# mLSTM exponentials between broadcast copies, and old-state products of two heads in turn

## The reference

```
dmat = where(causal, b[t] - b[s] + li[s], -inf)
inter = b + m
m_t = maximum(inter, max(dmat))
a = exp(dmat - m_t) * (q @ k.T)
num = exp(inter - m_t) * (q @ C) + a @ v
den = exp(inter - m_t) * (q @ n) + sum(a)
h = num / maximum(abs(den), exp(-m_t))
```

## Time and profile before

| | us |
|---|---|
| median of the timed runs | 2559.96 (one run of 2558.49) |
| the profiled execution | 2559.59 |
| its span in the trace | 2557.8 |
| PE busy | 2479.5 (97% of the span) |
| DVE, ACT, POOL busy | 1115.5, 827.9, 1349.7 |

### The profile page before, as it was taken

How to read it: one execution, slowest core, us unless ns; L and a number is a source line. 1 busy time by engine, 2 the same in 40 slices (tenths; PEclk the granted TensorE clock), 3 DMA queues, 4 the chain that set the end, 5 groups by cost and what they waited for, 6 DMA issues and landing times.

```text
span 2557.8 us, 41382 instructions
## 1 busy us (share of the span) xinstructions
PE 2479.5 (97%) x17104; PEld 2327.7 (91%) x17104; DVE 1115.5 (44%) x1610; ACT 827.9 (32%) x1517; POOL 1349.7 (53%) x635
## 2 busy tenths in 40 slices
PE   5999999999999999999989999999999999999997
PEld 3989976888999999999978999679899999999997
DVE  4443375534355423132564526653353463222235
ACT  3261355435422303021223513553454122112031
POOL 2645530445566666666656356016445666666664
PEclk9999999999999999999999999999999999999999
DMA  6202234531122222222211022442111222222221
GB/s 268 75 19 74 77 108 166 197 107 42 50 75 75 66 76 75 75 78 74 79 60 58 30 80 78 148 149 79 61 44 59 75 71 78 75 76 75 75 75 58
DMA packets 62619, 214.63 MB, mean 84 GB/s; under 512 B 6816, under 2 KB 11360, under 8 KB 62176
## 3 DMA queue, kind: packets, MB, share of 16 engines
q1 hardware_dynamic: 56160, 202.92, 23.5%
q10 hardware_dynamic: 6272, 9.07, 1.0%
HBM read 207.14 MB, written 4.49 MB: 83 GB/s over the span
## 4 chain that ended last, share of the span: by engine, by line
PE 92%; DVE 3%; ACT 1%; DVEq 1%; DMA 1%; issue 1%; SPq 1%; POOL 0%; POOLq 0%; ACTq 0%
PE big L567 22%; PE big L570 22%; PE big L571 22%; PE four L753 6%; PE big L828 2%; PE big L776 2%; PE four L649 2%; PE four L859 2%; PE four L974 2%; PE four L840 2%; PE four L798 1%; PE big L595 1%; PE big L599 1%; PE big L598 1%; PE big L950 1%; DMA first_mod<-in_first 1%
## 5 line engine op out<-in xcount | busy, mean ns | idle before, releaser
L527 POOL TENSOR_TENSOR w_hi<-raw,cst 128x1024 fp32r<-128x1024 f32 (+1 forms) x286 | 547.9, 1916 | 1042.2 <-PE big L567 833.0
L530 POOL TENSOR_TENSOR w_lo<-raw,w_hi 128x1024 fp32r<-128x1024 f32 (+1 forms) x286 | 735.3, 2571 | 40.7
L567 PE MATMUL big<-act_hi,w_hi 128*128 128x320 f32 x2304 | 718.6, 312 | 5.1 <-ACT mo_th L1376 3.9
L570 PE MATMUL big<-act_lo,w_hi 128*128 128x320 f32 x2304 | 713.5, 310 | 0.0
L571 PE MATMUL big<-act_hi,w_lo 128*128 128x320 f32 x2304 | 713.4, 310 | 0.0
L567 PEld LDWEIGHTS big<-act_hi,w_hi 128*128 128x128 f32 x2304 | 434.1, 188 | 13.8 <-issue 10.6
L570 PEld LDWEIGHTS big<-act_lo,w_hi 128*128 128x128 f32 x2304 | 434.2, 188 | 1.1
L571 PEld LDWEIGHTS big<-act_hi,w_lo 128*128 128x128 f32 x2304 | 434.0, 188 | 0.0
L567 PE MATMUL big<-u_hi,w_hi 128*128 128x320 f32 (+1 forms) x1024 | 319.0, 312 | 1.9 <-DVE u_lo L2209 1.9
L570 PE MATMUL big<-u_lo,w_hi 128*128 128x320 f32 (+1 forms) x1024 | 317.5, 310 | 0.0
L571 PE MATMUL big<-u_hi,w_lo 128*128 128x320 f32 (+1 forms) x1024 | 317.1, 310 | 0.0
(11 more groups left out here) (328 smaller groups left out, 4060.5 us busy)
## 6 DMA issues: line engine op xcount, KB each, us to landing
raw<-in_w SPq DMA_DIRECT2D x366, 512.0 KB, 3.4
first_mod<-in_first SPq DMA_DIRECT2D x16, 512.0 KB, 15.7
x<-in_x ACTq DMA_DIRECT2D x1, 2560.0 KB, 12.7
out_y<-x SPq DMA_DIRECT2D x8, 320.0 KB, 2.6
cst<-in_const ACTq DMA_DIRECT2D x1, 1665.0 KB, 8.4
small<-in_small ACTq DMA_DIRECT2D x2, 437.0 KB, 8.9
out_C<-c_new ACTq DMA_DIRECT2D x2, 258.0 KB
v_d<-in_past ACTq DMA_DIRECT2D x2, 256.0 KB, 2.9
```

Of the source, the lines that this page charges most:

```text
L527: nc.gpsimd.tensor_tensor(w_hi[:, to, 0:n], raw[:, slot, 0:n], ones[:, 0:1].to_broadcast([P, n]), ALU.mult)
L530: nc.gpsimd.tensor_tensor(w_lo[:, to, 0:n], raw[:, slot, 0:n], w_hi[:, to, 0:n].bitcast(f32), ALU.subtract).then_inc(split_ready, 1)
L567: first = mm(ps, wh, ah, start=k == 0, stop=False)
L570: mm(ps, wh, al, start=False, stop=False)
```

## The change

On ACT the exponentials of group 0 no longer follow all the broadcast copies: exps(0,0), (0,1) and (0,2) each come ahead of one of the copies 3, 4 and 5, and exps(0,3) behind them. Gate tile 2 follows at once, then the copy of the floor columns, the state weights of group 1, exps(1,0) to (1,2), gate tile 3, and exps(1,3). On DVE products(0,0) move ahead of broadcast copy 5. On PE the old-state products leave `m_values`: a new function `old_state(g)` issues the eight of a group, the two heads in turn, ahead of the odd unit's values. The even unit's values are issued without them and its result is announced by `old_state`.

```diff
+                def old_state(g):
+                    d, pair = g % 2, g // 2
+                    if g:
+                        wait_slots(2 * g + 1)
+                    else:
+                        pe.wait_ge(bc_copied, l * 6 + 6)
+                    pe.wait_ge(qw_ready, l * 4 + g + 1)
+                    order = key_tiles(d)[0:4]
+                    for i in order:
+                        for n in (2 * g, 2 * g + 1):
+                            r = slice(64 * (n % 2), 64 * (n % 2) + 64)
+                            last = mm(num_slot(n, i), stage[r, g % 2, P * i:P * i + P], C0[r, 2 * d + pair, 0:DV_M + 1],
...
+                            if n % 2 == 0 and i == order[3]:
+                                last.then_inc(num_ready, 1)
...
                     m_scores(g, 3)
+                    old_state(g - 1)
                     m_values(2 * g - 1)
                 project(l, USE["acq"], FIRST_BLOCK["acq"], 1, KD, act_hi, act_lo)
                 m_values(6)
+                old_state(3)
                 m_values(7)
...
                 output_gate(1)
-                for i in range(3, 6):
-                    keep_backward(i)
+                for i in range(3):
+                    exps(0, i)
+                    keep_backward(3 + i)
+                exps(0, 3)
+                output_gate(2)
                 act.wait_ge(ecol_ready, l + 1)
...
-                for i in range(4):
-                    exps(0, i)
-                output_gate(2)
+                weights_of_state(1)
+                for i in range(3):
+                    exps(1, i)
                 output_gate(3)
-                for i in range(4):
-                    exps(1, i)
-                weights_of_state(1)
+                exps(1, 3)
...
-                for i in range(6):
+                for i in range(5):
                     keep_broadcast(i)
-                for i in range(4):
+                products(0, 0)
+                keep_broadcast(5)
+                for i in range(1, 4):
                     products(0, i)
```

More of the change, by code:

```diff
@@ L952, in m_scores, with wait_slots @@
                     last.then_inc(ready[b], 1)
+                def wait_slots(n):
+                    d = unit(n)[1]
+                    pe.wait_ge(num_added if d == 0 else num_read, l * H_M + unit(n - 2)[2] + 1)
                 def m_values(n):
@@ L956, in m_values @@
                     r = slice(par, par + 64)
-                    if n == 1:
-                        pe.wait_ge(bc_copied, l * 6 + 6)
                     if n == 0:
@@ L961, in m_values @@
                         pe.wait_ge(ecol_copied, l + 1)
-                    if n >= 2:
-                        pe.wait_ge(num_added if d == 0 else num_read, l * H_M + unit(n - 2)[2] + 1)
-                    pe.wait_ge(qw_ready, l * 4 + g + 1)
+                    if n >= 2 and n % 2 == 0:
+                        wait_slots(n)
                     A = ea[:, n % 4, :]
                     order = key_tiles(d)[0:4]
-                    for i in order:
-                        mm(num_slot(n, i), stage[r, g % 2, P * i:P * i + P], C0[r, 2 * d + pair, 0:DV_M + 1],
-                           start=i == 3 or i == order[d], stop=False)
                     for at, i in enumerate(order):
@@ L973, in m_values @@
                             a = E_AT[d][j] + CTX + P * i - span(d, j)[0]
-                            mm(num_slot(n, i), A[:, a:a + P], vm[:, j + 1, h, 0:DV_M + 1], start=False,
-                               stop=j == i == 2 - 2 * d)
+                            mm(num_slot(n, i), A[:, a:a + P], vm[:, j + 1, h, 0:DV_M + 1],
+                               start=n % 2 == 0 and at in (0, 3 - 2 * d) and j == order[0],
+                               stop=n % 2 == 1 and j == i == 2 - 2 * d)
                     a = E_AT[d][LATE]
@@ L978, in m_values @@
                     pe.wait_ge(kw_ready, l * UNITS + 2 * g + 2)
-                    mm(num_slot(n, 5), kw[:, g, :], vm[:, 0, h, 0:DV_M + 1], start=False, stop=True)\
-                        .then_inc(num_ready, 1)
+                    last = mm(num_slot(n, 5), kw[:, g, :], vm[:, 0, h, 0:DV_M + 1], start=False, stop=n % 2 == 1)
+                    if n % 2:
+                        last.then_inc(num_ready, 1)
[11 more added lines that the diff above has]
+                            last = mm(num_slot(n, i), stage[r, g % 2, P * i:P * i + P], C0[r, 2 * d + pair, 0:DV_M + 1],
+                                      start=n % 2 == 1 and (i == 3 or i == order[d]),
+                                      stop=n % 2 == 0 and (i == 3 or i == 2 - 2 * d))
+                            if n % 2 == 0 and i == order[3]:
+                                last.then_inc(num_ready, 1)
                 def turn_head(h):
```

## The result

The changed kernel takes 2543.88 us (median of four runs, 2543.29 to 2544.47) where the kernel before took 2559.96. The ratio is 0.9937, with a 95% interval of 0.9925 to 0.9948: 16 us or 0.6% faster, and 0.1 us from the forecast of 2544. The interval leaves out 1 by far, so a gain of this size can be told from no change, although the prediction counts anything under 2% as the same. One execution of the kernel before (6258.39 us) and one of experiment 5 (7428.82 us), both far slower than all others, are left out of the medians.

What follows compares the result with a forecast made beforehand. PE bounds the kernel, carrying 92% of the chain that ended last, so time is won in its waits, clock or matmul cycles. 2559.6 - 13.0 - 7.7 + 5.2 = 2544.1, forecast 2544 us, range 2538 to 2553.

Steps and rivals of the forecast that it cites:

- Term 1: Start of the mLSTM loop: earlier exps(0,0) and tanh remove PE's waits and lost clock between gate tiles 2 and 3; 13.0 us gained.
- Both waits and the half clock: Old start, per layer: PE waits 1.7 us for DVE's buffer release, 2.0 for the tanh; clock 0.50 at 147 to 148 us.
- Term 2: PE's group loop: old-state products of two heads in turn overlap, 1.00 us per group for 1.96; 7.7 us gained.
- Term 3: Third group: DVE's divisors and additions delay buffers, PE waits ahead of scores(3,0) to (3,3); 2.6 us per layer, 5.2 lost.
- The unsure neighbourhood: Group 1's key weighting on DVE beside POOL's masks and split: up to 1.3 us per layer could come back; taken as nothing.
- (a): Group loop: DVE takes back all of Term 2, PSUM reading perhaps the bottleneck, only the start is won; 2546.6 us, chance 0.14.
- (b): PE's old-state products don't overlap, so Term 2 is nothing and Term 3 stays; 2551.8 us, chance 0.08.
- (c): Start: exps(0,0) come late or the tanh of tile 2 stays behind something, half of Term 1 lost; 2550.6 us, chance 0.07.
- (d): Ahead of scores(3,0) to (3,3) the clock falls, 5 us each: one per layer 2554, chance 0.08; two 2564, chance 0.02.
- (e): Group loop: DVE has room after all, most of Term 3 is not paid; 2540 us, chance 0.07.

Runs made afterwards that it cites:

- experiment 5: The changed kernel without DVE's additions of h out of the slots for units 2 and 3 (two backward heads stay incomplete); 2540.49 us, ratio 0.9922.
- Experiments 6 and 7: Kernel before, tanh of gate tile 2 ahead of exps(0,1) to (0,3): 2551.85 us; kernel before, exps(0,0) and products(0,0) put ahead of broadcast copies: 2554.99 us.
- experiment 4: The changed kernel with DVE's divisors and additions of units 2 and 3 each put behind the products that free score buffers; 2540.64 us, ratio 0.9925.
- Experiment 2: The kernel before with only PE's part of the change, old-state products of both heads in turn, ACT's and DVE's order kept; 2559.44 us, ratio 0.9997.
- experiment 3: The changed kernel with old_state issuing four products of one head, then four of the other; 2548.25 us, ratio 0.9955.

## Why the prediction was right

**Term 1** (13.0 us): 12.8 measured, and by the mechanism named. Exps(0,0) took a place where ACT stood idle: copy 3 began on ACT 3.60 us behind scores(0,0) (128.19 - 124.59), as before (129.58 - 125.98). Both waits and the half clock are gone in both layers. The stretch is 8.09 us for the 7.98 foreseen. Experiments 6 and 7 show that the old loss isn't a sum of two waits. The starts gained 7.0 and 5.8 us (layers 0 and 1) without both waits, 5.3 and 2.6 without the second alone, 2.8 and 1.6 without the first alone: one wait alone could still take the clock down, and how much that cost varied from layer to layer.

**Term 2** (7.7 us): right in size and in its mechanism, the overlap of two heads. Four groups at 1.00 for 1.96 are 3.84 us per layer; the loop without the additions is 47.99 - 44.68 = 3.3 us shorter than before, with 0.6 still lost around scores(3,1) in experiment 5, together 3.9. That the four groups share it evenly is not so: from scores(2,0) to the even unit's values it is 157.39 - 155.68 = 1.71 us after, and was 167.54 - 164.95 = 2.59, 0.88 less and not 0.96, since the change to 128 rows now comes right behind the scores. The last group, between projection tiles, won more, about 1.3. The upper bound of the term comes to 8.3, not 8.4.

**Term 3** (5.2 us): right in place, and nearly in size. The brackets ahead of scores(3,0) to (3,3) are 0.58, 0.54, 0.40 and 0.52, 2.04 us per layer for the 2.6 foreseen. They don't show all the time lost. From unit 3's last product to unit 4's first value product it is 168.27 - 164.79 = 3.48 us; in experiment 4, where nothing waits there, 167.53 - 165.51 = 2.02: 1.46 us for brackets of 1.12. The reason is likely that scores of two buffers that run apart no longer overlap; no run takes that by itself. With scores(3,2) and (3,3) (2.56 for 1.30 at the same place of group 1) the loss is 2.7 per layer. Experiments 4 and 5 name the cause from both sides: later or absent additions take the waits away.

**The unsure neighbourhood**, taken at nothing, cost nothing: the weighting of group 1's keys came at 154.73, 0.4 us after POOL's split had ended (152.00 + 2.36), and took 0.25 us. Experiment 2 shows what it would have cost, 0.8 us per layer.

**Rivals.** (a) fell: DVE took back 2.7 of 3.9 us per layer, not all. What it named, the reading of PSUM, is where the loss lies, but DVE had time left: with the same work in another order (experiment 4) 1.6 of the 2.7 are gone. (b) fell: the products overlap in pairs (experiment 3). (c) fell with the starts of 19.25 us. (d) fell: the clock was 1.00 from 144 to 190 us and from 1408 to 1428, through the four waits of 0.40 to 0.58. Its price of 5 us a fall was also too dear, with 1.3 to 1.5 measured for a fall behind a single wait and at most 3.5 with two. (e) fell as to the order as it is; with DVE's order changed it came true at 2540.64.

What the sum leaves out is the 1.1 us outside the mLSTM. The terms add to 2544.1 and the profiled execution took 2543.29: that the median agrees to 0.1 us owes something to chance.

## What to carry to other kernels

Read a stall with a clock loss behind it as one item: its parts aren't additive, and a second wait while the clock is low can cost more than its own length (here 5.3 and 2.6 us came back for a wait of 1.97). Where PE gets faster, ask next what stands on the reading engine's queue ahead of the release that PE needs; here a reordering of DVE's queue, with no work saved, gave another 3.2 us. A change in one stage can pay in another through an engine that nobody waits for: POOL's masks, which run earlier by the new start, no longer fall beside DVE's key weighting.

## What was not expected of the hardware

The same wait of 1.70 us at the same place cost the clock in layer 1 and not in layer 0 of one execution (0.50 against 1.00 in the windows behind it). Matmuls 64 rows deep with 129 columns pass at 1.00 us for eight when they go to the two halves of the partitions in turn, 1.54 when four of one half follow four of the other, and 1.96 when values stand between them; matmuls of the two halves start 0.007 us apart, those of one half 0.11. A key weighting of 64 columns on DVE takes 0.25 us alone, and beside POOL's work 0.50, 0.73 or 1.07, each time ending within 0.06 us of POOL's instruction.
